# The first two modulation vectors of a transformer block made in four quarters of two tiles instead of two halves of four

## The reference, cut to what matters

```python
mod = jax.nn.silu(c) @ w_ada[l] + b_ada[l]                 # c: 1 x 1024, w_ada: 1024 x 6144
shift1, scale1, gate1, shift2, scale2, gate2 = jnp.split(mod[:, None, :], 6, axis=-1)
h = rms_norm(x, norm1_w[l]) * (1 + scale1) + shift1        # 512 x 1024
proj = h @ w_in[l]                                         # the first of many products
```

## Time and profile before

| | us |
|---|---|
| median of 3 runs (lowest, highest) | 2318.69 (2316.74, 2318.97) |
| the profiled execution's own time | 2318.61 |
| its span | 2316.8 |
| TensorE busy in the span | 2247.6 (97%) |
| from the start to the last matmul of "ab" | 63.1 |

### The profile page before, as it was taken

One profiled execution on the slowest core, in us unless ns is written; L12 is line 12 of the kernel. 1 busy time (PEld: TensorE's weight loads), 2 busy tenths in 40 slices (PEclk: granted clock), 3 DMA queues, 4 the chain that ended last, 5 costly groups with the idle time before them and its releaser, 6 DMA issues.

```text
span 2316.8 us, 26615 instructions
## 1 busy us (share of the span) xinstructions
PE 2247.6 (97%) x10800; PEld 1840.7 (79%) x10800; DVE 1099.7 (47%) x1589; ACT 959.7 (41%) x1399; POOL 676.9 (29%) x399
## 2 busy tenths in 40 slices
PE   7999999999999999999999999999999999999998
PEld 6778788986777787888887788788777878888876
DVE  5666544556544335444312879633454153332334
ACT  4755553235454335333322342445554243332334
POOL 1133223003012262322222222221333353332334
PEclk7999999999999999999999999999999999999999
DMA  8522221112122244343333523232222423333332
GB/s 290 151 86 73 62 57 55 55 42 55 50 78 66 72 145 137 116 128 111 96 92 95 145 82 92 78 100 87 78 69 64 134 85 91 109 91 92 108 100 91
DMA packets 347982, 220.63 MB, mean 95 GB/s; under 512 B 18393, under 2 KB 327244, under 8 KB 347860
## 3 DMA queue, kind: packets, MB, share of 16 engines
q1 hardware_dynamic: 338462, 202.31, 29.8%
q10 hardware_dynamic: 9398, 16.62, 2.2%
HBM read 210.49 MB, written 8.41 MB: 94 GB/s over the span
## 4 chain that ended last, share of the span: by engine, by line
PE 86%; DVE 7%; ACT 4%; issue 1%; POOL 1%; DMA 1%; ACTq 0%; SPq 0%; DVEq 0%
PE ps L351 84%; DVE arena L380 2%; PE ps L354 2%; DVE arena L372 2%; ACT arena L369 1%; DVE scr L380 1%; ACT whi L369 1%; ACT scr L369 1%; ACT L360 1%; POOL hlo L372 0%; ACT L369 0%; DVE arena L377 0%; DMA wraw<-in_w_in_dram 0%; DMA arena<-in_x_dram 0%; DVE wlo L372 0%
## 5 line engine op out<-in xcount | busy, mean ns | idle before, releaser
L372 POOL TENSOR_TENSOR wlo<-wraw,whi 128x1024 fp32r<-128x1024 f32 (+1 forms) x159 | 383.2, 2410 | 1088.0 <-ACT whi L369 1087.8
L369 ACT ACTIVATE whi<-wraw 128x1024 fp32r<-128x1024 f32 (+1 forms) x328 | 340.8, 1041 | 331.8 <-PE ps L351 281.1
L351 PE MATMUL ps<-hhi,whi 128*128 128x512 f32 x1664 | 438.8, 403 | 20.2 <-ACT hhi L369 7.3
L351 PE MATMUL ps<-hlo,whi 128*128 128x512 f32 x1664 | 421.0, 392 | 1.9 <-POOL hlo L372 1.8
L351 PE MATMUL ps<-hhi,wlo 128*128 128x512 f32 x1664 | 419.3, 391 | 0.8 <-POOL wlo L372 0.8
L351 PEld LDWEIGHTS ps<-hhi,whi 128*128 128x128 f32 x1664 | 309.5, 190 | 101.4 <-issue 25.5
L351 PEld LDWEIGHTS ps<-hlo,whi 128*128 128x128 f32 x1664 | 314.5, 189 | 70.2 <-POOL hlo L372 2.9
L351 PEld LDWEIGHTS ps<-hhi,wlo 128*128 128x128 f32 x1664 | 313.0, 188 | 66.5 <-POOL wlo L372 1.3
L372 DVE TENSOR_TENSOR wlo<-wraw,whi 128x1024 fp32r<-128x1024 f32 (+1 forms) x169 | 217.7, 1289 | 293.9 <-ACT whi L369 293.6
L351 PE MATMUL ps<-arena 128*128 128x128 f32 (+3 forms) x2016 | 280.5, 292 | 9.3 <-ACT arena L369 6.3
L351 PEld LDWEIGHTS ps<-arena 128*128 128x128 f32 x2016 | 245.0, 191 | 28.4 <-ACT arena L369 8.3
(11 more groups left out here) (201 smaller groups left out, 2569.0 us busy)
## 6 DMA issues: line engine op xcount, KB each, us to landing
wraw<-in_w_in_dram SPq DMA_DIRECT2D x99, 512.0 KB, 3.8
wraw<-in_w_ff_dram SPq DMA_DIRECT2D x64, 512.0 KB, 4.2
wraw<-in_ffn_w_up_dram SPq DMA_DIRECT2D x44, 512.0 KB, 3.9
wraw<-in_w_gate_dram SPq DMA_DIRECT2D x32, 512.0 KB, 4.3
arena<-in_w_ada_dram SPq DMA_DIRECT2D x20, 512.0 KB, 3.9
arena<-in_w_ada_dram SPq DMA_DIRECT2D x8, 1024.0 KB, 11.4
wraw<-in_ffn_w_down_dram SPq DMA_DIRECT2D x16, 512.0 KB, 4.1
wraw<-in_w_branch_dram SPq DMA_DIRECT2D x16, 512.0 KB, 3.4
```

Of the source, the lines that this page charges most:

```text
L351: return pe.e.matmul(o, l, r, start=start, stop=stop)
L369: return ac.e.activation(o, i, f, bias=bias, scale=scale, **kw)
L372: return q.e.tensor_tensor(o, a, b, op)
```

## The change

The two vectors are made in four quarters s = 0..3 of 256 columns of each vector. Quarter s serves k = 2s and 2s + 1.

- **Loads.** `load_ada(s)` is four DMAs of 512 KB with rows of 1 KB (before: 1 MB, rows of 2 KB). Quarter 0 comes in front of the three weight blocks of "ab", quarters 1 to 3 behind them. The two DMAs of one p share a semaphore, so each user waits for both; only the last pair (s = 3, p = 1) has one each.
- **TensorE.** Two one-column matmuls for each row tile instead of four; the row tiles on TensorE are four for both vectors of quarter 0 and two and three for the others. Quarter 0 is summed in front of `turn_x(2)` and `turn_x(3)`. In the "ab" loop quarters 1, 2 and 3 are summed at k = 2, 4 and 6, in front of `lows(k - 1)`, with `highs(k)` behind them. `turn_x(4)` to `turn_x(7)` are at k = 1, 3, 5, 5.
- **VectorE.** No copies of `xt`. Instructions of 256 columns. The first share of quarter 1 stands in front of `first_mod(0)`; then for s = 1, 2, 3: the lows of tiles 2s - 2 and 2s - 1, the second vector's share of quarter s, the first vector's share of quarter s + 1, `first_mod(s)`.
- **ScalarE** copies all eight `xt` tiles, and issues the `xs1` DMA in front of `first_h(6)`, behind the last load of `w_ada`.
- **GpSimd** makes the low parts of tiles 0, 2 and 4, between its two weight blocks and the constants.

```diff
-        ADA_PE = [[(1, 3, 5, 7), (7,)], [(3, 7), (7,)]]
+        ADA_PE = [[(1, 3, 5, 7), (1, 3, 5, 7)], [(3, 7), (3, 5, 7)], [(3, 7), (3, 5, 7)], [(3, 7), (3, 5, 7)]]
...
-        H1 = Split("h1", HP, lambda k: "ve")
+        H1 = Split("h1", HP, lambda k: "po" if k in (0, 2, 4) else "ve")
...
-                            if l.X is H1 and k == 4:
-                                lows(3)
-                                self.between(4)
-                                highs(4)
+                            if l.X is H1 and k in (2, 4, 6):
+                                self.between(k)
+                                lows(k - 1)
+                                highs(k)
                                 continue
...
             def between(self, k):
...
-                if k == 4:
+                if k == 1:
+                    self.turn_x(4)
+                if k == 3:
+                    self.turn_x(5)
+                if k == 5:
+                    self.turn_x(6)
                     self.turn_x(7)
-                    bk = self.mod_open(1)
...
+                if k in (2, 4, 6):
+                    s = k // 2
+                    bk = self.mod_open(s)
+                    self.mod_part(bk, s, 0, 0)
+                    self.mod_part(bk, s, 0, 1)
+                    self.mod_part(bk, s, 1, 0)
+                    self.mod_sum(bk, s, 0)
+                    self.mod_part(bk, s, 1, 1)
+                    self.mod_sum(bk, s, 1)
...
-                for k in range(4, 8):
+                for k in range(8):
                     ac.wait_ge(*at("st_mm", "xt", k))
                     act(XT[k], PA.of("xt", k)[:, :], ACT.Copy).then_inc(*inc("st_act", "xt", k))
...
                 self.mod_part(0, 1, 1)
+                self.mod_part(1, 0, 0)
                 self.first_mod(0)
-                self.ahead(0)
-                self.first_low(0)
-                self.first_low(1)
-                self.mod_part(1, 0, 0, (0, 1))
-                self.first_low(2)
-                self.mod_part(1, 0, 0, (2, 3))
-                self.first_low(3)
                 self.mod_part(1, 0, 1)
-                self.mod_part(1, 1, 0)
-                self.mod_part(1, 1, 1)
-                self.first_mod(1)
-                for k in range(4, 8):
-                    self.first_low(k)
+                for s in range(1, 4):
+                    if s == 1:
+                        self.ahead(0)
+                    self.first_low(2 * s - 2)
+                    self.first_low(2 * s - 1)
+                    self.mod_part(s, 1, 0)
+                    self.mod_part(s, 1, 1)
+                    if s < 3:
+                        self.mod_part(s + 1, 0, 0)
+                        self.mod_part(s + 1, 0, 1)
+                    self.first_mod(s)
+                self.first_low(6)
+                self.first_low(7)
...
+                for k in range(0, 6, 2):
+                    po.wait_ge(*at("st_act", "h", k))
+                    self.low(H1, k, HS[k % 3])
                 po.wait_ge(SG.sem("cst2"), 16)
...
+        def ada_in(s, p, g):
+            if s == 3 and p == 1:
+                return SG.sem(f"ada_in31{g}"), 16
+            return SG.sem(f"ada_in{s}{p}"), 32
```

More of the change, by code:

```diff
@@ L389, in build @@
         CROW = A[0:8, 55, 0:P]
[L390 to L391 removed]
+        ADA0 = [[A[:, 21 + 8 * s + 4 * p:25 + 8 * s + 4 * p, :].rearrange("p a (b c) -> p (a b) c", b=2) for p in range(2)]
+                for s in range(4)]
+        ADA_PE = [[(1, 3, 5, 7), (1, 3, 5, 7)], [(3, 7), (3, 5, 7)], [(3, 7), (3, 5, 7)], [(3, 7), (3, 5, 7)]]
         SQ4, RX = SM[:, 424:428], SM[:, 428:432]
@@ L1194, in mod_part @@
                     if k // 4 == g:
-                        pe.wait_ge(SG.sem(f"ada_in{s}{p}{g}"), 16)
-                        for c in range(4):
-                            mm(bk[:, 4 * p + c:4 * p + c + 1], ADA0[s][p][:, k, c * P:(c + 1) * P], SC[:, k:k + 1],
+                        pe.wait_ge(*ada_in(s, p, g))
+                        for c in range(2):
+                            mm(bk[:, 2 * p + c:2 * p + c + 1], ADA0[s][p][:, k, c * P:(c + 1) * P], SC[:, k:k + 1],
                                not self.opened, False)
@@ L1202, in mod_sum @@
                 pe.wait_ge(*at("m0_ve", s, p))
-                for c in range(4):
-                    t = mm(bk[:, 4 * p + c:4 * p + c + 1], ADA0[s][p][:, 0, c * P:(c + 1) * P], ones[:, 0:1],
-                           not self.opened, p == 1 and c == 3)
+                for c in range(2):
+                    t = mm(bk[:, 2 * p + c:2 * p + c + 1], ADA0[s][p][:, 0, c * P:(c + 1) * P], ones[:, 0:1],
+                           not self.opened, p == 1 and c == 1)
                     self.opened = True
@@ L1803, in prologue @@
                 for k in range(1, 8):
-                    if k == 4:
-                        for p in range(2):
-                            ac.wait_ge(SG.sem(f"ada_in1{p}1"), 16)
-                        ac.wait_ge(*at("st_ve", "xt", 3))
+                    if k == 6:
+                        ac.wait_ge(*ada_in(3, 1, 0))
+                        ac.wait_ge(*ada_in(3, 1, 1))
                         ac.wait_ge(*at("st_act", "xt", 7))
@@ L2543, in prologue @@
             def prologue(self):
-                for k in range(4):
-                    ve.wait_ge(*at("st_mm", "xt", k))
-                    cp(ve, XT[k], PA.of("xt", k)[:, :]).then_inc(*inc("st_ve", "xt", k))
                 self.mod_part(0, 0, 0)
@@ L3547, in load_ada @@
                     sp.e.dma_start(ADA0[s][p][:, 4 * g:4 * g + 4, :],
-                                   rows(D["w_ada"][0], 4 * g, 4, p * 1024 + s * S, S)).then_inc(SG.sem(f"ada_in{s}{p}{g}"), 16)
+                                   rows(D["w_ada"][0], 4 * g, 4, p * 1024 + 256 * s, 256)).then_inc(ada_in(s, p, g)[0], 16)
         def load_late(p, k):
@@ L3554, in load_late @@
                     sp.wait_ge(*at("ma_mm", "s", h, 3))
-            sp.wait_ge(*(at(*before) if before else at("ada_mm", "c", 1)))
+            sp.wait_ge(*(at(*before) if before else at("ada_mm", "c", 3)))
             sp.e.dma_start(ADA_RAW[slot], D["w_ada"][0, k * P:(k + 1) * P, p * 1024:(p + 1) * 1024]).then_inc(
@@ L3573, in sync_program @@
                 load_block(u)
-            load_ada(1)
+            for s in range(1, 4):
+                load_ada(s)
             sp.wait_ge(*at("st_po", "rz"))
```

34 lines of the change are left out of this document (13 added, 21 removed).

## The result

The changed kernel took 2325.81 us (median of 7, 2322.12 to 2327.12), the kernel before beside it 2318.49 (7, 2316.00 to 2318.97): a ratio of 1.0032 with an interval of 1.0021 to 1.0042, so + 7.3 us. The forecast was 2321.9 with a range of 2315.5 to 2326.7. The time lies inside the range, but on the slower side, where rival D stood (2325.7), and not within 0.2% of before, which had been the likeliest. That it meets D's total is luck: D has all of its + 7 at the end of "ab", where + 4.8 was measured, and 2.5 came behind it. The profiled execution took 2327.12, with a span of 2325.3.

The account below looks back on a forecast made before the run. TensorE, busy 97% of the span, bounds the kernel, so what delays it counts. The end of "ab" moves from 63.1 to 66.3; + 3.2 on 2318.7 gives 2321.9 us, range 2315.5 to 2326.7.

Parts of the forecast that it names:

- rival D: In "ab": one-column bundles lower the clock in the middle of each quarter; + 6 to + 8, 2325.7 us; chance 28%.
- Part 1: Start, quarter 0: fewer one-column instructions, gated by x and a DMA wait; mod 0 at 28.2, a gain of 1.8.
- the new gate: Start: `first_mod(0)` stands on VectorE behind quarter 1's first share, which waits for two DMAs; 28.2 against 29.98.
- Part 2: Quarter 1: VectorE's chain, with + 2.0 from GpSimd's turns, makes mod 1 ready at 40.7; bounds 38.7 to 41.
- Part 3: Quarter 2: VectorE's chain of 9.5 sets mod 2 at 50.2; TensorE needs 7.5 at 2.4 GHz, 15 at 1.2.
- Part 4: Quarter 3: TensorE later than VectorE's 56.4, so mod 3 at 59.7; 3.0 more at the low clock.
- Part 5: End of "ab": after mod 3 come high 6, 18 matmuls and 4 transposes, ending at 66.3, 6.6 behind mod 3.
- The count that the prediction made as a check: TensorE alone: 40 one-column instructions in the loop become 84, + 4.7 at 0.107 or + 9.4 at 0.214; start returns 1.8.
- The planned sum: End of "ab" moves from 63.1 to 66.3: + 3.2 us.
- Costed at nothing: Later rows and `cst2`, GpSimd's later `sel`, `xs1` issued at 53 and `first_h(6)` behind a load wait: all priced at zero.
- No gap at k = 7: Sign: a matmul gap at k = 7, from rows arriving late, would have shown the forecast wrong.
- One to one: Behind "ab": the shift of its end passes in full to the total, everything later as before, only moved.

Follow-up runs that it names:

- second profile: Changed kernel, unchanged, profiled and timed once more: median 2325.44 us, 1.0033 against the kernel before beside it.
- run 4: Changed kernel with all low parts on VectorE and none on GpSimd: 2324.87 us in one execution.
- run 1: Changed kernel without TensorE's row tiles of quarters 1 to 3 (sums incomplete), 60 one-column instructions less: 2322.23 us in one execution.
- run 2: Changed kernel with only VectorE's first and last shares kept in quarters 1 to 3 (sums incomplete): 2325.71 us in one execution.
- run 3: Changed kernel with each `first_mod` on VectorE ahead of the next quarter's shares, nothing left out: 2326.37 us in one execution.
- run 12: Changed kernel with `first_mod` ahead of next quarter's shares and 20 instead of 28 one-column instructions in each of quarters 1 to 3: 1.0018, median 2323.52 us.
- second pair: Both kernels, unchanged, profiled once more on one chip: profiled executions of 2320.01 us before and 2325.44 us after.
- run 11: Kernel before with 44 more one-column instructions on TensorE, 16 at k = 2 and 28 at k = 6: 2324.60 us in one execution.
- run 7: Kernel before with each 1 MB load cut into two of 512 KB with rows of 1 KB: 2322.26 us in one execution.
- run 5: Kernel before with 8 chained fills on VectorE in front of `first_mod(1)`, a delay of 5.3 us: 1.0023, + 5.3 us.
- run 6: Kernel before with 4 chained fills on VectorE in front of `first_mod(1)`, a delay of 2.65 us: 1.0012, + 2.8 us.
- run 9: Kernel before, unchanged, profiled once more: median 2320.20 us, 1.0005 against its other runs there; profiled execution 2320.01 us.

## Why the prediction was right or wrong

| | forecast | after | second profile |
|---|---|---|---|
| mod 0 ready | 28.2 | 28.4 | 26.9 |
| mod 1 | 40.7 | 40.3 | 38.9 |
| mod 2 | 50.2 | 51.4 | 50.0 |
| mod 3 | 59.7 | 60.8 | 59.4 |
| end of "ab" | 66.3 | 68.0 | 66.7 |
| against before | + 3.2 | + 4.8 | + 5.3 |

("Ready" is the start of `first_mod` and 0.36 us.)

**Part 1 was right in mechanism and size.** ACT's copies are done at 17.5 (forecast 17.6), the scaling at 19.6 (19.8), and a first share of quarter 1 that waits for its DMA stands ahead of `first_mod(0)` as said: [2.92 <-DMA]. Loads with rows of 1 KB run at 349 GB/s:

```profile
DMA packets 2106, 2.09 MB, mean 349 GB/s; under 512 B 64, under 2 KB 2106, under 8 KB 2106
```

(after, 26 to 32 us; forecast 355 between the two of the earlier trace rows.) The Trainium skill (DMA: Bandwidth & Descriptors, Specifications) gives line rate from 512 B up; by the trace 1 KB is still a tenth short of the 386 GB/s that 2 KB have the earlier trace rows. The gain of 1.8 was a difference to one execution, and it is 1.6 in the first pair and 1.2 in the second. Over all profiles it holds: mod 0 was ready at 28.1 to 30.0 in the seven with before's prologue (29.3 on average), at 26.7 to 28.4 in the five with after's order (27.3). In each of these five the first share of quarter 1 waits 2.3 to 2.9 for its DMA, so the new gate is on the path; in four of them nothing else holds `first_mod(0)`.

**Part 2 was right (40.7, measured 40.3), with less behind it than it says.** VectorE's chain does set quarter 1 in after, and it and GpSimd do take turns: low 1 took 1.52, where the earlier trace rows have 0.68, and the next TENSOR_SCALAR 1.36, where the earlier trace rows have 0.35. That is + 1.8, and the forecast had + 2.0. The Trainium skill (SBUF - State Buffer, SBUF: two separate sides) calls the shared port pair an exclusive lock, held for a full instruction, for which a VectorE operation contends in a 2-port performance mode, or with two SBUF inputs when GpSimd reads SBUF; the rows agree for the two inputs. TENSOR_SCALAR with one 256-column input was held as well, and no run shows in which mode it ran. Of the 2.0 the weight block was to cost 1.1 and low 0 the other 0.9; run 4 has 1.1 for low 0, of which 0.7 comes back as work that VectorE doesn't do. And TensorE is only about 1 us ahead of VectorE here, so that ending the turns alone could win no more than that.

**Part 3 failed: the term of TensorE.** Forecast was VectorE's chain of 9.5 with TensorE at 7.5 behind it. VectorE was a little quicker, 9.2 with its `first_mod` (its last share ends at 49.2), as run 1 confirms, where this chain sets the quarter and takes 9.17; and TensorE took 11.0. The low clock from 40.0 to 46.8 lay on nine 512-column products and four transposes: 4.86 us from 41.92 to 46.78, where 9 x 0.23 + 4 x 0.11 make 2.5. That is + 2.4 for TensorE; with its wait of 1.10 for high 2, which the 7.5 had left out, it makes about the 11.0. 1.8 of it shows as the wait of `first_mod(2)`. The prediction had the price (15 at the low clock) but took the high clock for this quarter. That was rival D, with one correction: D expected the bundle itself at 0.214, and saw its price there. In after only the last few of one bundle ran so; the products behind it did. In runs 2, 3, 4 and 12 a part of one bundle did run at 0.214, so D's mechanism exists as well.

**Part 4 was right** (9.5 forecast, 9.4), by TensorE as said, and with 2.03 of waiting on DVE in place of 2.8. **Part 5 was short by 0.6:** from mod 3 to the end 7.2 instead of 6.6, because products from 60.26 to 63.9 ran at the low clock (9 in 3.74). **The whole of "ab".** From mod 0 ready to the end it is 33.2 before and 39.7 after (33.25 and 39.73 in the second pair): + 6.5. The 44 instructions are 4.7 of it; the rest is about the clock: TensorE is busy at 1.2 GHz for 16.1 us instead of 12.6, and half of these 3.5 is 1.8 (an estimate, from the first pair). Runs 1 and 11 show the bundles as the cause from both sides: without the row tiles 3.8 of it go, and with them two of the three stretches of low clock; 44 one-column instructions put into before bring + 4.8, their bare time. The count that the prediction made as a check (+ 44 instructions, 4.7 at 0.107) was its best number. The planned sum took off 1.8 for the start, and the clock behind the bundles ate that.

**Costed at nothing:** right. No gap at k = 7, no wait for rows, `xs1` at 53.7; in the kernel before the smaller loads cost nothing (run 7).

**One to one** was right for the delays (runs 5 and 6). What the sum left out is what comes behind; "behind it everything as before, moved" was not met in the first pair. The medians say + 7.3 and + 6.9, the end of "ab" + 4.8 and + 5.3. Over 14 profiles the way from the end of "ab" to the last matmul is 2245.0 to 2250.6, for the same work. With 10 to 17 us of low clock on it (five profiles) it is 2245.0 to 2246.9, with 20 to 31 (nine) it is 2246.8 to 2250.6. The seven kernels made from before average 2247.0, the seven from after 2248.4, each with a spread of over 4 us. In 49 executions of before the mean granted clock was 0.990, in 12 of after 0.987; within before alone those at 0.993 average 2316.8 (6), those at 0.987 average 2321.2 (4). So the 2 us above the + 5 go with a lower clock (T4); at 0.987 alone after averages 2325.9 (5) against these 2321.2, + 4.7. The lower clock itself is no accident of single executions: nine of the twelve of after are at 0.987 or 0.986, of the 49 of before four are at 0.987 and none is lower. A part of it lies ahead of the end of "ab" in the second pair (27.3 us against 20.5). Why it comes with this change is not shown: in the second pair the tails are equal, the intervals reach down to + 4.6, and the delay of 5.3 us, which adds no work on TensorE, also had a low mean clock, 0.988. So "it belongs to no edit" is not shown either, and this stays open.

## What to carry to other kernels

Where one engine is busy 97% of the time, a finer split of a sum is paid in its instructions: each additional one-column product stood on the path at its full 0.107 us, whatever was won ahead of it. Price some of the work BEHIND a bundle of tiny products at the low clock too, for there it fell in most quarters here: about 1.8 us of the 6.5 that "ab" became longer by. Read a vector's moment from the END of what makes it: a start 3.9 us earlier was 1.9 us in truth, because a second instruction was held up. And where two engines' chains are within 1 or 2 us of each other, relieving one can show nothing: taking most of VectorE's shares away won 0.0, taking TensorE's away 3.8 of 6.4.

## What the runs showed of the hardware

- In after, its second profile and runs 2 to 4 there are 15 bundles of 28 one-column instructions. The granted clock fell to the 1.2 GHz level behind ten of them, at most 1.2 us after their end, and within the other five, in three of these for the last few instructions only. Three 512-column products then took 1.45 to 1.65 us instead of 0.85 to 0.95. With the row tiles taken out (run 1) there was no such fall in quarters 2 and 3.
- With one and the same prologue the first vector is ready anywhere in a range of 2 us (28.1 to 30.0), and the 2245 us behind "ab" took 3.3 us longer in one of two profiles of before. One profile of each kernel can't size a change of 3 us; from mod 0 ready to the end of "ab", by contrast, both kernels came back within 0.05 us.
- A TENSOR_SCALAR of 256 columns took 1.36 us instead of 0.35 while GpSimd made a low part of 512. A SCALAR_TENSOR_TENSOR of 4 columns took 2.19 instead of 0.16 beside GpSimd's weight block (run 9).
